# A two-layer hybrid backbone: per-tile normalisation inside the query/key stage, and modulation rows in four column groups

## The reference, cut to what matters

```python
def adaln_in(x, cond, w, b, g):
    m = jax.nn.silu(cond) @ w + b
    shift, scale, gate = jnp.split(m[:, None, :], 3, axis=-1)
    return rms_norm(x, g) * (1 + scale) + shift, gate
...
    a_q, a_k, a_v, a_g, b_q, b_k, b_v, b_r, b_g = split_cols(h @ w_in, EVEN_SIZES)
    q = rms_norm(a_q.reshape(B, T, A_HEADS, HD), qn)
    k = rms_norm(a_k.reshape(B, T, A_KV, HD), kn)
```

## Time and profile before

| | |
|---|---|
| median of 3 runs | 2386.4 us (2386.39 to 2391.01) |
| the profiled execution | 2388.93 us, its span 2387.1 us |
| busy: PE, PE weight loads, DVE, ACT, POOL | 2066.8, 1331.8, 950.3, 770.2, 162.2 us |
| chain that ended last | PE 76%, DVE 10%, ACT 5%, DMA 3% |
| mean granted TensorE clock | 0.921 of full speed |
| read from and written to HBM | 96.47 MB, 19.96 MB |

### The profile page before, as it was taken

The page is one execution under the profiler, slowest core; times in us unless marked ns, Lnnn a source line. Parts: engine busy times, 40 slices in busy tenths (PEclk is TensorE's granted clock), DMA queues, the critical chain, the costliest instruction groups (busy, mean ns, idle before and its releaser), DMA issues.

```text
span 2387.1 us, 29729 instructions
## 1 busy us (share of the span) xinstructions
PE 2066.8 (87%) x12020; PEld 1331.8 (56%) x12020; DVE 950.3 (40%) x1915; ACT 770.2 (32%) x1627; POOL 162.2 (7%) x235
## 2 busy tenths in 40 slices
PE   5697999998999989896989999967958958868998
PEld 1464555543556543673557764347548548457476
DVE  0566444302233364425443321362372372462442
ACT  0432444420222213324224551134234234323431
POOL 0000000000000000000000000014014014013000
PEclk9697999998999999996989999979969969969999
DMA  6101000021000124333010002100100000100323
GB/s 255 57 1 73 1 1 1 1 99 63 1 1 1 56 88 167 114 133 109 1 64 1 1 10 105 55 27 3 25 27 2 28 33 2 60 2 17 112 86 104
DMA packets 61289, 118.34 MB, mean 50 GB/s; under 512 B 5048, under 2 KB 27724, under 8 KB 61025
## 3 DMA queue, kind: packets, MB, share of 16 engines
q1 hardware_dynamic: 40033, 57.53, 7.4%
q0 software_dynamic: 8640, 33.75, 4.1%
q10 hardware_dynamic: 12480, 25.17, 2.9%
HBM read 96.47 MB, written 19.96 MB: 49 GB/s over the span
## 4 chain that ended last, share of the span: by engine, by line
PE 76%; DVE 10%; ACT 5%; DMA 3%; POOL 3%; DVEq 2%; issue 2%; ACTq 1%; SPq 0%; PEldq 0%; PEld 0%; POOLq 0%
PE ps L523 8%; PE ps L1730 8%; PE ps L806 8%; PE ps L974 5%; PE ps L917 5%; PE ps L280 4%; PE ps L1301 3%; PE ps L1326 3%; PE ps L1141 2%; PE ps L1142 2%; PE ps L1143 2%; PE ps L761 2%; PE ps L1918 2%; PE ps L788 2%; PE ps L787 2%; PE ps L775 2%
## 5 line engine op out<-in xcount | busy, mean ns | idle before, releaser
L806 PE MATMUL ps<-work 128*128 128x512 f32 (+3 forms) x512 | 231.1, 534 | 0.0
L830 DVE TENSOR_REDUCE work<-ps 128x1 f32<-128x512 f32 (+2 forms) x272 | 145.3, 562 | 198.1 <-PE ps L761 197.4
L523 PE MATMUL ps<-wring,hT 128*128 128x512 f32 (+2 forms) x576 | 195.7, 499 | 12.9 <-DMA work<-in_knorm_a 7.9
L1730 PE MATMUL ps<-hT,wring 128*128 128x512 f32 (+1 forms) x576 | 190.6, 493 | 8.0 <-SPq L2083 5.6
L880 ACT ACTIVATE work<-ps 128x512 f32<-128x512 f32 (+3 forms) x256 | 132.1, 517 | 192.7 <-PE ps L788 141.7
L787 PE MATMUL ps<-qA,kA 128*128 128x512 f32 (+3 forms) x256 | 171.3, 669 | 2.3 <-ACT work L871 1.9
L523 PEld LDWEIGHTS ps<-wring,hT 128*128 128x128 f32 x576 | 109.9, 193 | 94.0 <-issue 85.6
L1730 PEld LDWEIGHTS ps<-hT,wring 128*128 128x128 f32 x576 | 96.1, 193 | 103.4 <-issue 99.9
L974 PE MATMUL ps<-wring,hT 128*128 128x512 f32 x288 | 127.3, 605 | 5.3 <-SPq L1520 3.4
L917 PE MATMUL ps<-hT,wring 128*128 128x512 f32 (+1 forms) x384 | 126.9, 492 | 4.0 <-DVEq L184 4.0
L761 PE MATMUL ps<-kA,qA 128*128 128x128 f32 (+3 forms) x336 | 101.1, 351 | 28.6 <-DVE work L830 14.8
(11 more groups left out here) (289 smaller groups left out, 3574.4 us busy)
## 6 DMA issues: line engine op xcount, KB each, us to landing
work<-in_w_mod ACTq DMA_DIRECT2D x10, 2048.0 KB, 13.2
work<-in_x_sample SPq DMA_DIRECT2D x16, 512.0 KB, 6.6
wring<-in_w_in_even POOLq DMA_DIRECT2D x4, 2048.0 KB, 8.5
out_y_sample<-work SPq DMA_DIRECT2D x16, 512.0 KB, 3.0
work<-out_y_sample SPq DMA_DIRECT2D x16, 512.0 KB, 4.9
wring<-in_w_in_odd POOLq DMA_DIRECT2D x3, 2048.0 KB, 8.7
wring<-in_w_in_odd POOLq DMA_DIRECT2D x12, 512.0 KB, 6.6
yA_gated<-work SPq DMA_DIRECT2D x8, 576.0 KB, 2.8
```

Of the source, the lines that this page charges most:

```text
L523: mm = pe.matmul(ps[:, 2 * (t % 2) + b, 0:n], hT[:, k, t * P:(t + 1) * P], w[:, k, :], start=(k == 0), stop=(k == KD - 1))
L806: pe.matmul(ps[:, 5 + c_, (qa - q0) * P:(qb - q0) * P], vaug[:, h // 4, kt, :], pT[i % 3][:, 0:(qb - qa) * P], start=(first and l == 0), s ...
L830: v.tensor_reduce(dst, src, AX.X, ALU.max).then_inc(sm("mx_used"), 1)
L1730: mm = pe.matmul(ps[:, PROJ_BANK[n], 0:m], w[:, k, b * P:(b + 1) * P], hT[:, k, o:o + m], start=(k == 0), stop=(k == KD - 1))
```

## The change

The stage ada goes. Its tiles are made inside qkv, two tiles ahead of the one that is projected: before the loop tiles 0 and 1, in the loop tile t+2 behind the projection of tile t. In layer 0 the statistics and the scaling of tiles 0 and 1 and the transposes of tile 0 stand in mod0, ahead of the modulation rows. Transposed tiles have one set of two banks (6 and 7), so a tile's transposes wait for the writes of the tile ahead; DVE and ACT write 4 of 8 each. The transposes of q and k have one set of banks (4 and 5) too. The loads of the norm weights and caches follow mod0. The modulation rows are four pieces of 256 columns, which write the PSUM partitions from 0, 32, 64 and 96 on; they are copied out in four copies, and in `gates_dve` the bias is added in a pass of its own. The buffers of x move to places that are free then. In the delta stages five semaphores become two, with waits on the same events.

```diff
         def rows_pe(pe, w, bank):
-            for j in range(2):
-                for k in range(KD):
-                    mm = pe.matmul(ps[0:2, bank + j, :], scv[:, k, :], w[j][:, k, :], start=(k == 0), stop=(k == KD - 1))
+            for k in range(KD):
+                for q in range(4):
+                    mm = pe.matmul(mod_quarter(bank, q), scv[:, k, :], w[q // 2][:, k, 256 * (q % 2):256 * (q % 2) + 256],
+                                   start=(k == 0), stop=(k == KD - 1))
             return mm
+        def mod_quarter(bank, q):
+            return ps[32 * q:32 * q + 2, bank + q // 2, 256 * (q % 2):256 * (q % 2) + 256]
...
-            v.tensor_copy(mod_row(stage)[0:2, :].rearrange("p (a n) -> p a n", a=2), ps[0:2, bank:bank + 2, :]).then_inc(sm("mrow"), 1)
+            for q in range(4):
+                mm = v.tensor_copy(mod_row(stage)[0:2, 256 * q:256 * q + 256], mod_quarter(bank, q))
+            mm.then_inc(sm("mrow"), 1)
...
         def mod_pe(pe):
+            ada_turn_pe(pe, 0, 0)
             pe.wait_ge(sm("cond_silu"), 1)
...
         def mod_act(act):
+            act.preload_act_table_set(EXP_LN)
+            ada_first_act(act, 0)
...
         def mod_dve(v):
+            ada_first_dve(v, 0)
             v.wait_ge(sm("cond_silu"), 1)
...
         def gates_dve(v, l):
-            v.tensor_tensor(grow[0:2, :].rearrange("p (a n) -> p a n", a=2), ps[0:2, 2:4, :],
-                            gb2[0:2, :].rearrange("p (a n) -> p a n", a=2), ALU.add).then_inc(sm("gate_rows"), 1)
+            for q in range(4):
+                v.tensor_copy(grow[0:2, 256 * q:256 * q + 256], mod_quarter(2, q))
+            v.drain()
+            v.tensor_tensor(grow[0:2, :], grow[0:2, :], gb2[0:2, :], ALU.add).then_inc(sm("gate_rows"), 1)
...
+        def ada_turn_pe(pe, l, t):
+            pe.wait_ge(sm("xh_done"), NT * l + t + 1)
+            if t:
+                pe.wait_ge(sm("hT_act"), NT * l + t)
+                pe.wait_ge(sm("hT_dve"), NT * l + t)
+            for k in range(KD):
+                mm = pe.transpose(xT_ps(k), a_xh[t % 2][:, k * P:(k + 1) * P], ident)
+            mm.then_inc(sm("xT_ps"), 1)
...
         def qkv_pe(pe, l):
+            pe.wait_ge(sm("qkv_in"), qkv_in_count(l))
+            pe.transpose(ps[:, 5, 128:256], ck, ident).then_inc(sm("ckT_ps"), 1)
+            for t in range(1 - l, AHEAD_X):
+                ada_turn_pe(pe, l, t)
...
+                if t + AHEAD_X < NT:
+                    ada_turn_pe(pe, l, t + AHEAD_X)
                 if t >= 1:
                     u = t - 1
                     pe.wait_ge(sm("qkr_done"), NT * l + u + 1)
-                    if u >= 2:
-                        pe.wait_ge(sm("qkT_done"), NT * l + u - 1)
+                    if u:
+                        pe.wait_ge(sm("qkT_done"), NT * l + u)
...
         def qkv_act(act, l):
+            if l:
+                ada_first_act(act, l)
+            ada_evac_act(act, l, 0)
             for t in range(NT + 1):
+                if t + AHEAD_X < NT:
+                    ada_stats_act(act, l, t + AHEAD_X)
+                if t + AHEAD_X - 1 < NT:
+                    ada_evac_act(act, l, t + AHEAD_X - 1)
...
         def qkv_dve(v, l):
+            v.wait_ge(sm("ck_high"), l + 1)
+            keys_low(v, ps[:, 5, 128:256], CTX).then_inc(sm("ck_done"), 1)
...
             for t in range(NT):
+                if t + AHEAD_X < NT:
+                    ada_scale_dve(v, l, t + AHEAD_X)
+                if t + AHEAD_X - 1 < NT:
+                    ada_evac_dve(v, l, t + AHEAD_X - 1)
```

More of the change, by code:

```diff
@@ L312, in mod_pe @@
             pe.transpose(ps[:, 0, 0:48], vecs[0:48, :], ident[0:48, 0:48]).then_inc(sm("vecT_ps"), 1)
+            ada_turn_pe(pe, 0, 0)
             pe.wait_ge(sm("cond_silu"), 1)
-            columns_pe(pe, "mod0", 1, [weights(pe, f"mod0.{j}") for j in range(2)], 1)
+            columns_pe(pe, "mod0", 1, [weights(pe, f"mod0.{j}") for j in range(2)], 0)
             pe.drain().then_inc(sm("w_used"), 2)
-            columns_pe(pe, "mod0", 2, mod_weights(pe, "mod0"), 4)
+            columns_pe(pe, "mod0", 2, mod_weights(pe, "mod0"), 3)
             phase_end(pe)
@@ L353, in gates_dve, with xT_ps @@
                                 gpost_b.rearrange("p (a n) -> p a n", a=2), ALU.mult)
-        ar = Region()
         NX = 3
-        a_x = [ar.take(D) for _ in range(NX)]
-        a_xh = [ar.take(D) for _ in range(2)]
-        a_junk = ar.take(D)
-        a_st = [ar.take(4) for _ in range(2)]
-        def xT_ps(t, k):
-            b, j = (0, k) if k < 4 else (1, k - 4) if k < 6 else (2, k - 6)
-            return ps[:, 3 * (t % 2) + b, j * P:(j + 1) * P]
+        AHEAD_X = 2
+        def xT_ps(k):
+            return ps[:, 6 + k // 4, (k % 4) * P:(k % 4 + 1) * P]
         def x_rows(l, t):
@@ L421, in ada_evac_dve, with ada_first_act, ada_first_dve @@
             cnd = int(t == NS)
-            for k in range(6):
-                mm = v.tensor_scalar(hT[:, k, t * P:(t + 1) * P], xT_ps(t, k),
+            for k in range(4):
+                mm = v.tensor_scalar(hT[:, k, t * P:(t + 1) * P], xT_ps(k),
                                      mods[:, 1, k, cnd:cnd + 1], mods[:, 0, k, cnd:cnd + 1], ALU.mult, ALU.add)
             mm.then_inc(sm("hT_dve"), 1)
-        def ada_pe(pe, l):
-            for t in range(NT):
-                pe.wait_ge(sm("xh_done"), NT * l + t + 1)
-                if t >= 2:
-                    pe.wait_ge(sm("hT_act"), NT * l + t - 1)
-                    pe.wait_ge(sm("hT_dve"), NT * l + t - 1)
-                for k in range(KD):
-                    mm = pe.transpose(xT_ps(t, k), a_xh[t % 2][:, k * P:(k + 1) * P], ident)
-                mm.then_inc(sm("xT_ps"), 1)
-            phase_end(pe)
+        def ada_turn_pe(pe, l, t):
[6 more added lines that the diff above has]
+            mm.then_inc(sm("xT_ps"), 1)
+        def ada_first_act(act, l):
+            for t in range(AHEAD_X):
+                ada_stats_act(act, l, t)
+        def ada_first_dve(v, l):
+            for t in range(AHEAD_X):
+                ada_scale_dve(v, l, t)
         R65 = slice(0, HD + 1)
@@ L468, in backbone @@
         wqk = qr.take(128)
+        ar_ = Region(at_qkv - 4 * T)
+        a_x = [ar_.take(D) for _ in range(NX)]
+        a_xh = [ar_.take(D)]
+        ar_ = Region(qr.at)
+        a_xh.append(ar_.take(D))
+        a_junk = ar_.take(D)
+        a_st = [ar_.take(4) for _ in range(2)]
         ar2 = Region(at_qkv)
@@ L492, in qkv_sp @@
         def qkv_sp(sp, l, n):
-            phase_seen(sp, n)
+            if l:
+                phase_seen(sp, n)
+            for t in range(NX):
+                ada_load(sp, l, t)
+            if l == 0:
+                sp.dma_start(con[:, FIRST:], consts[:, FIRST:]).then_inc(sm("rest_in"), 16)
+                phase_seen(sp, n)
             d = sm("qkv_in")
@@ L500, in qkv_sp @@
                 sp.dma_start(wqk[:, HD:2 * HD], knorm_a[0].partition_broadcast(P)).then_inc(d, 16)
+            for t in range(NX, NT):
+                ada_load(sp, l, t)
             ko, vo = ((new_attn_k, new_attn_v), (new_swa_k, new_swa_v))[l]
@@ L527, in qkv_pe @@
                         pe.drain().then_inc(sm("w_used"), 2)
-                if t == 0:
-                    pe.transpose(ps[:, 7, 128:256], ck, ident).then_inc(sm("ckT_ps"), 1)
+                if t + AHEAD_X < NT:
+                    ada_turn_pe(pe, l, t + AHEAD_X)
                 if t >= 1:
@@ L2147, in backbone @@
         eps_col = cst("eps")
-        STAGES = ["mod0", "ada0", "qkv0", "att0", "gateA0", "gla", "gateB0", "fin0",
-                  "ada1", "qkv1", "att1", "gateA1"]
+        STAGES = ["mod0", "qkv0", "att0", "gateA0", "gla", "gateB0", "fin0",
+                  "qkv1", "att1", "gateA1"]
         STAGES += [f"{s}{h}" for h in range(4) for s in ("dpre", "dsys", "dscan")]
@@ L2231, in _ @@
                     mod_act(act)
[L2232 to L2234 removed]
+                else:
+                    act.preload_act_table_set(EXP_LN)
                 qkv_act(act, l)
```

109 lines of the change are left out of this document (46 added, 63 removed).

## The result

| | before | after |
|---|---|---|
| median (its runs) | 2388.7 us (2386.39 to 2392.87) | 2318.8 us (2316.38 to 2322.14) |
| ratio, 95% interval | | 0.9703 (0.9691 to 0.9715) |
| the profiled execution, its span | 2388.9, 2387.1 us | 2322.1, 2320.3 us |

The change takes 69.9 us off, where 80.8 had been worked out: 12.8 us above the forecast of 2306, inside its range. The two profiled executions differ by 66.8 us; that of after is the slowest of its four runs, 3.3 above their median.

What follows compares the result with a forecast made beforehand. DVE was taken to bound normalisation, PE the qkv stage, with all six modulation row groups on the path. The terms summed to -80.8 us, from 2388.9 to 2308 profiled and 2306 as a median, range 2294 to 2338.

Steps and rivals of the forecast that it cites:

- Step 1: Modulation rows: four column groups side by side take 3.6 us against 13.9, copies 1.4; a row group gives 10.1 us.
- The rival of two at a time: Modulation rows: only two column groups run together, each of six row groups takes 3.4 us more: 2326; chance 0.11.
- The rival of weight loads in the open: Modulation rows: 64 weight loads stand between the matmuls, 5.8 us a group: 2341; chance 0.03.
- no overlap: Modulation rows: column groups do not overlap, a row group is 13.9 us again, the merged stage is left: 2365; chance 0.06.
- Step 2: Layer 0 to the end of mod0: modulation ready at 42.1 against 62.1, -20.0 us, with 1.7 us for half speed.
- step 6: Gates of both layers: shorter row group, less +1.5 us for four copies and a separate addition: -8.8 and -8.7 us.
- Step 3: Layer 0, modulation to first projection: 12.0 us against 35.1, -23.1, with small loads at 6.4 us beside the projection weights.
- Step 4: Inside qkv: eight transposes between projections add 6.1 us in each layer, period 11.74 us, no wait for DVE.
- The fourth rival: qkv loop: DVE's writes come 1 us late in each tile, 18 us at most: 2324; chance 0.06.
- The rival that ends slower: qkv loop: PE's clock falls to half speed, 10.3 us more for each of 18 projections: 2490; chance 0.03.
- Step 5: Tails of qkv: last q/k transposes wait for the previous tile's remainders, +2.1 us in layer 0, +2.9 in layer 1.
- Steps 7 and 8: gateB0's row group -10.0 us, fin0's -9.0; layer 1 ahead of its first projection 16.2 us against 34.6, -18.4.

Runs made afterwards that it cites:

- its repair: Changed kernel with the last tile's q/k transposes in the two banks that normalisation no longer needs: 2312.0 us, ratio 0.969.
- the experiment on the bias: Changed kernel with the gate's bias added in the four copies out of PSUM, without a pass of its own: 2314.2 us, ratio 0.9691.
- the kernel with fillers alone: Changed kernel plus unread matmuls on PE, 18 ahead of mod0's rows and four in each gates' pause: 2317.8 us, ratio 0.9712.
- the last kernel above: Changed kernel with last q/k transposes in free banks, early small loads, bias added in the copies, and unread matmuls keeping PE busy: 2293.2 us, ratio 0.9612.

## Why the prediction came out as it did

**Step 1, rows in four groups: right.** 3.64 us at full speed, 3.6 taken. The earlier trace rows had shown two groups; four behave alike. The rival of two at a time (2326, 0.11) falls with the 7.04 us that two really take; it predicted 6.9. The Trainium skill's 2.38 times for three groups ("TensorE: Matmul & The Clock Gate", the section on packing small matmuls) would have given 5.8 us, as an estimate; the trace shows 13.89/3.64 = 3.8 times for four groups, and no run here has three. The rival of weight loads in the open (2341, 0.03) is false: 64 loads and 64 matmuls lie in 3.64 us, all with one row group. The sentence of the Trainium skill that the prediction named there (same page, the section on the mechanism: a weight load overlaps with matmuls in flight only when its row group differs) does not hold for this shape; the prediction left out that the same section also lets a load into the background weight buffer be pulled ahead, and no run here shows which buffer these took. That of no overlap (2365, 0.06) is false too, but with the loops in the other order the time comes near it: 2361. The copies took 1.71 us, four at 0.43, where 1.4 was taken of a bound of 1.8: 0.3 in each of six places.

**Step 2, -20.0, was -16.9.** The term mis-sized is the 1.7 us for half speed. It had been read from the difference of two groups of 15 us, the first of which came up to full speed after some 3.5 us. The packed group stayed at half speed for nearly all of its 6.36 us, and the second began there, behind 2.7 us with nothing but the 0.65 of the columns, which I had put down as harmless: 1.1 and 1.6 us more than worked out. The copies and columns behind each add 0.4 and 0.2. With step 6 (3.8 us over both layers) this is the largest error. The busy time by stretch, after (columns as in the earlier trace rows):

```profile
34.30:36.90 2.60, 0.65 (x8) 0.57 (x8) 1.72 (x5) 0.00 (x0) 0.00 (x0) 0.99 0.00 0
36.90:42.20 5.30, 5.26 (x64) 1.81 (x64) 0.13 (x1) 0.00 (x0) 1.76 (x2) 0.68 0.65 217
```

**Step 3, -23.1, was -21.7.** The chain behind the loads was right within 0.1 us (5.57 from L522 to the first projection, 5.6 worked out). The loads took 7.8 us, 6.4 taken. The term left out the x loads issued behind them: with those held back the loads took 6.4, projection weights and all, and with them but without the weights 7.8.

**Step 4, +6.1 in each layer: right.** The period is 11.74, the clock of this loop 0.95 in layer 0 and 0.96 in layer 1. The fourth rival (the loop waits at DVE) is false, and its margin was judged well: DVE's write of a tile ends at 91.11 + 1.37 = 92.48, and PE goes to that bank at 92.93, 0.45 us later. The rival that ends slower, a clock that falls in the loop, is false by the clock row:

```profile
58.60:176.30 117.70, 106.10 (x390) 65.98 (x389) 77.91 (x172) 59.59 (x164) 1.75 (x2) 0.95 0.15 55
...
1058.40:1178.30 119.90, 108.20 (x391) 66.02 (x390) 63.99 (x150) 50.35 (x137) 3.55 (x4) 0.96 0.15 50
```

What I had not counted: the first projection, straight behind transposes, takes 11.57 us where 13.48 stood behind an idle wait. That is the 1.9 us by which qkv of layer 0 came out better.

**Step 5, tails: right.** +2.2 in layer 0 against +2.1; measured twice, by the trace and by its repair. In layer 1 it is 10.3 us from the last transposes but one to the first scores before the change, 13.5 after it and 10.3 with the repair: +3.1 against +2.9. So the traces have 5.3 us for both layers, 5.0 worked out. The repair gave 6.8 us by medians and 3.1 by the ratios, which does not contradict it.

**Step 6, gates, -8.8 and -8.7, were -6.8 and -6.9.** The term left out is the clock of what follows. Behind 3.19 us of pause L352 takes 5.58 us, before 3.91. Behind the long row group and 1.38 us L352 still ran fast; behind the packed one and 1.90 (the experiment on the bias) it fell in part. Is it the shorter group or the longer pause? The kernel with the other order of issue has a long group, 11.40 us, and a pause of 3.16 us, and its L352 took 6.34 us. So a long group does not save it behind such a pause. With a long group and 1.38 us it took 3.91 before, and 4.62 in the kernel with the merged stage alone. The pause is the larger part, as far as single traces tell. The longer pause itself is 3.19 - 1.38 = 1.8, where 1.5 was taken.

**Steps 7 and 8.** gateB0 -9.7, -10.0 worked out: right. From fin0's group on, -25.5 in place of -27.4. The modulation was ready 7.1 us after the group's start, 7.3 worked out:

```profile
1039.82 0.18 DVE L311 SCALAR_TENSOR_TENSOR mods<-mods,vecsT 128x16 f32<-128x16 f32 x1
```

From there to L522 at 1048.69 it is 8.7 us, for which step 8 had 6.6 of loads; the chain behind it, to the first projection at 1058.36, is 9.7, 9.6 worked out. So the loads alone were mis-sized, by 2.1 us.

**Stages that nobody edited** took 2.8 us more in fin0 and 3.2 in layer 1's attention. The second in the clock rows, before and after, at the same work:

```profile
1260.00:1280.00 20.00, 19.69 (x102) 13.97 (x102) 6.25 (x11) 9.76 (x21) 0.00 (x0) 1.00 0.00 1
```
```profile
1196.90:1216.90 20.00, 19.69 (x85) 13.20 (x84) 5.44 (x10) 7.81 (x16) 0.00 (x0) 0.82 0.00 0
```

PE is busy for the same 19.69 us, but starts 85 records in place of 102, at a clock of 0.82. Of 20 us, 0.18 is 3.6. In the thirteen traces of this case that attention with its gateA, from qkv's last transposes to the row group, took 257.4 to 262.3 us (before 259.1, after 260.9), and the way from gateB0's row group to fin0's 117.4 to 123.5 (before 120.0, after 123.3). So these 6.0 us are within what the stages vary by from trace to trace. Whether the change tilts them (both the shortest and the longest of these times are of kernels with the merged stage) is open.

The account, then: 14.0 us of shortfall by the profiles are 3.1 (mod0), 1.4 (loads), 2.0 + 1.8 (gates), 1.9 (fin0's group to layer 1), 0.3 (gateB0) and 6.2 (unedited stages), less 1.9 and 0.8 in the two qkv stages. By the medians it is 10.9.

## What to carry to other kernels

A matmul with a stationary operand of few columns can have four of them side by side in PSUM, at partitions 0, 32, 64 and 96: here each row group went from 13.89 to 3.64 us. They must be issued in turn, one step of each group after the other; group by group, most of it is lost (11.40).

Where a packed group replaces a long one, look at the clock of what follows: the pause behind it stays, and the eight matmuls after it went from 3.91 to 5.58 us here. A small load's time also depends on what is issued behind it (6.4 or 7.8 us), and one that waits for nothing belongs ahead of the barrier (10.4 us here by medians, 6.5 by the ratios).

## What the runs showed of the hardware

PE starts matmuls of another column group ahead of their turn, but by three records only. Issued in turn, four groups overlap throughout, 3.64 us; group by group, four pairs of records do at each border, 11.40 us in all. I had expected either 3.6 to 5 us or 13.9.

A group of packed matmuls can fall to half speed in its middle. In the last kernel above, the first group of mod0 began with a round of four records each 0.215 us, went to 0.427 a round after some 0.5 us, and came back near 4.0, by the starts of its records. PE had idled 3.03 us ahead of it. The row of that stretch:

```profile
28.30:33.80 5.50, 5.32 (x64) 2.19 (x64) 0.00 (x0) 0.00 (x0) 0.00 (x0) 0.69 1.04 382
```

The group's clock was the same 0.69 as that of the changed kernel's second group (0.68), which was cold from its start. The extents of mod0's two groups in the traces with this code lie between 3.64 and 6.57 us for the first and 3.63 and 5.33 for the second, most of them with no edit near. In four of the nine the second group ran at full speed throughout, in three of these behind the same 2.7 us.

Early in the program the granted clock reads 1.00 where the records run at half pace: the first group of mod0, 6.36 us long, against 3.64 in the kernel with fillers alone. The busy time of both in that stretch, changed kernel first:

```profile
27.90:29.00 1.10, 1.10 (x12) 0.41 (x16) 0.00 (x0) 0.00 (x0) 0.00 (x0) 1.00 1.04 384
```
```profile
27.90:29.00 1.10, 1.06 (x20) 0.56 (x24) 0.00 (x0) 0.00 (x0) 0.00 (x0) 1.00 1.05 387
```

PE worked on 12 records in the one and on 20 in the other, at the same reading. In the changed kernel the trace's first record of the clock stands at 33.5 us, where the pace of the records doubles, so the 1.00 ahead of it is not a measurement. There the pace of the records is to be believed.
